# Prompt attention: the scores of a head pair on row groups of TensorE, and the order of the work around them

## The reference, cut to what matters

```python
q = (c_q @ p['w_q_b']).reshape(B, T, MLA_HEADS, QK_NOPE + QK_ROPE)
q_nope = q[..., :QK_NOPE]                  # 64 per head
q_pe = rope(q[..., QK_NOPE:], pos)         # 32 per head
q_lat = einsum('bthn,chn->bthc', q_nope, p['w_uk'])
s = (einsum('bqhc,bkc->bhqk', q_lat, ckv) + einsum('bqhr,bkr->bhqk', q_pe, kpe)) * ATTN_SCALE
s = where(k_pos <= q_pos, s, -inf)         # causal
p = softmax(s, axis=-1)
o_lat = einsum('bhqk,bkc->bqhc', p, ckv)   # then times w_uv, per head
```

## Time and profile before

| | us |
|---|---|
| median of 3 runs (lowest, highest) | 3310.39 (3306.4, 3311.9) |
| the profiled execution's own time | 3304.57 |
| its span | 3302.7 |
| prompt attention, layer 0: first scores / end of the last outputs | 927.68 / 1120.4 |
| the same stage of layer 1: first scores / last outputs begin | 2561.8 / 2754.2 |

### The profile page before, as it was taken

The page is one execution under the profiler, slowest core; times in us unless marked ns, Lnnn a source line. Parts: engine busy times, 40 slices in busy tenths (PEclk is TensorE's granted clock), DMA queues, the critical chain, the costliest instruction groups (busy, mean ns, idle before and its releaser), DMA issues. The chain is left out here.

```text
span 3302.7 us, 68611 instructions
## 1 busy us (share of the span) xinstructions
PE 3234.5 (98%) x29405; PEld 2317.0 (70%) x29405; DVE 1990.4 (60%) x3892; ACT 944.2 (29%) x2025; POOL 146.5 (4%) x168
## 2 busy tenths in 40 slices
PE   8999999999999999999999999999999999999999
PEld 5887875656666677766988878756666666777688
DVE  5545345666556778744875544466665567786565
ACT  4101013334356422221131010133333564222201
POOL 1000000000000122100000000000000001221000
PEclk8999999999999999999999999999999999999999
DMA  8122211111220377676121222111112204775431
GB/s 262 32 54 74 73 53 43 52 45 52 58 72 17 117 278 271 228 252 243 58 80 41 52 75 71 53 43 47 48 52 66 59 11 174 276 272 218 162 137 55
DMA packets 252274, 357.17 MB, mean 108 GB/s; under 512 B 47203, under 2 KB 221597, under 8 KB 243398
## 3 DMA queue, kind: packets, MB, share of 16 engines
q1 hardware_dynamic: 220166, 184.94, 18.6%
q0 software_dynamic: 15168, 151.07, 12.4%
q10 hardware_dynamic: 16640, 16.78, 1.6%
HBM read 302.17 MB, written 48.35 MB: 106 GB/s over the span
## 5 line engine op out<-in xcount | busy, mean ns | idle before, releaser
L1453 PE MATMUL ring<-u,stream_ring 128*128 128x364 f32 (+1 forms) x1728 | 613.5, 487 | 2.5 <-PEq L1324 2.5
L1453 PEld LDWEIGHTS ring<-u,stream_ring 128*128 128x128 f32 x1728 | 303.7, 189 | 150.2 <-issue 8.5
L2883 PE MATMUL dec_s_bank<-u,att_q_rows 32*64 32x256 f32 x8192 | 245.0, 386 | 0.4 <-ACT att_q_rows L2931 0.4
L2883 PEld LDWEIGHTS dec_s_bank<-u,att_q_rows 32*64 32x64 f32 x8192 | 186.8, 135 | 40.2 <-issue 12.5
L2940 ACT ACTIVATE page_probs<-dec_s_bank,dec_minus_top 128x1024 f32<-128x1024 f32 x64 | 71.4, 1115 | 338.7 <-DVE dec_minus_top L2977 338.7
L2974 DVE TENSOR_REDUCE dec_group_top<-dec_s_bank 128x1 f32<-128x1024 f32 x64 | 78.4, 1225 | 123.6 <-PE dec_s_bank L2883 123.6
L2528 PE MATMUL attn_s<-u 96*128 96x512 f32 (+3 forms) x384 | 146.2, 490 | 6.2 <-issue 3.4
L2958 DVE STREAM_TRANSPOSE u<-dec_ckv 128x2048 f32<-128x2048 f32 x52 | 116.9, 2285 | 0.7 <-DMA dec_ckv<-in_cache_mla_ckv_dram,page_row 0.7
L2166 ACT ACTIVATE rwkv_inv_x<-rwkv_inv_t 64x128 f32<-64x128 f32 x192 | 59.1, 308 | 193.4 <-DVE rwkv_inv_t L2341 191.8
L2666 DVE TENSOR_TENSOR attn_s<-attn_s,tables 128x128 f32<-128x128 f32 x128 | 38.1, 298 | 118.7 <-PE attn_s L2528 118.7
L2616 ACT ACTIVATE attn_probs_t<-ring 128x512 f32<-128x512 f32 (+2 forms) x192 | 87.1, 489 | 71.3 <-PE ring L2537 69.7
(11 more groups left out here) (745 smaller groups left out, 6566.6 us busy)
## 6 DMA issues: line engine op xcount, KB each, us to landing
stream_ring<-in_w_in_dram SPq DMA_DIRECT2D x96, 512.0 KB, 4.2
merge_sig<-gates_feature_major SPq DMA_DIRECT2D x14, 1632.0 KB, 8.3
u<-in_w_ada_dram ACTq DMA_DIRECT2D x16, 1024.0 KB, 15.1
gates_feature_major<-rwkv_gate_stage SPq DMA_DIRECT2D x72, 182.0 KB, 1.9
gates_feature_major<-rw_raw_p SPq DMA_DIRECT2D x24, 272.0 KB, 2.7
gates_feature_major<-rwkv_gate_stage SPq DMA_DIRECT2D x36, 180.0 KB, 2.0
start_ada<-in_w_ada_dram SPq DMA_DIRECT2D x6, 1024.0 KB, 13.2
x_feature_major<-o_mla SPq DMA_DIRECT2D x2, 2176.0 KB, 9.8
```

Source lines behind the costliest of these rows:

```text
L1453: mm = pe.matmul(self.banks[j % 2][:, 0:m], self.stream.w(self.first + n - self.early, k), self.s.u[:, k, t0:t0 + m], start=(k == 0), stop ...
L2883: mm = pe.matmul(S[64 * half:64 * half + NQ, 512 * i:512 * i + NK], q, keys, start=(cb == 0), stop=(cb == BLOCKS))
```

## The change

Nothing of the mathematics changes. In words:

- The plain queries of both heads lie in one tile of 128 rows (head i in rows 64 i to 64 i + 63), the plain keys too. The rotary queries of each head lie twice, in rows 64 i + 32 part; the rotary keys lie four times, in 32 rows each.
- `scores(pair)` makes both heads. The keys are halved (`n` = half of them, 64 to 512). For each half, both heads' plain products go to rows 0 to 63 and 64 to 127 of the array (two row groups). Then four rotary products (2 heads x 2 halves) go to the four row groups of 32 and accumulate on the same banks. Half y of head i is in its own PSUM bank. Each rotary matmul increments `scored`: four a pair instead of two.
- `scores(pair)` waits for the exponentials of both tiles of the pair before it, and the order of all queues is by pairs.
- Four buffers `probs` instead of two; pieces one behind each pair, two behind pair 6.
- "uk" is two full transposes instead of four half ones, "lat" two matmuls of 128 rows instead of four of 64 rows (against `q_apart`, zero outside a head's rows); ACT keeps "q" and "k" with one copy instead of two, "uk" with half as many columns.
- SP spreads the rotary queries with 8 DMAs a round instead of 4, and `scores` waits for 128 counts. POOL's four key copies no longer wait for `rope`.

```diff
-    after_tile = {0: 2, 1: 2, 2: 1, 3: 1, 4: 1, 5: 1, 6: 1}
+    after_pair = {0: 1, 1: 1, 2: 1, 3: 1, 4: 1, 5: 1, 6: 2, 7: 1}
...
@@ block.sync: spread_rope
-                        for x in range(2):
-                            sp.dma_start(q_t[r % 2][i][NOPE + x * half:NOPE + (x + 1) * half, :],
-                                         roped_q[x][h * half:(h + 1) * half, :]).then_inc(rope_in[r % 2], 16)
+                        for part in range(2):
+                            at = rope_rows(i, part).start
+                            for x in range(2):
+                                sp.dma_start(q_rope[r % 2][at + x * half:at + (x + 1) * half, :],
+                                             roped_q[x][h * half:(h + 1) * half, :]).then_inc(rope_in[r % 2], 16)
...
@@ block.tensor: scores
-                def scores(a):
-                    ...
-                    if a >= 2:
-                        pe.wait_ge(exped, a - 1)
-                    for c in range(0, (qt + 1) * P, 512):
-                        n = min(512, (qt + 1) * P - c)
-                        mm = pe.matmul(S[a % 2][:, c:c + n], q_t[r % 2][i][0:QK, qt * P:(qt + 1) * P], k_t[r % 2][i][0:QK, c:c + n],
-                                       start=True, stop=True)
-                    mm.then_inc(scored, 1)
+                def scores(pair):
+                    r, qt, _ = tiles[2 * pair]
+                    x, n = r % 2, keys_in_half(2 * pair)
+                    ...
+                        pe.wait_ge(rope_in[x], 128 * (r // 2 + 1))
+                    ...
+                        pe.wait_ge(exped, 2 * pair)
+                    for part in range(2):
+                        keys = slice(part * n, (part + 1) * n)
+                        for i in range(2):
+                            rows = rows_of_head(i)
+                            pe.matmul(S[i][:, 512 * part:512 * part + n], q_plain[x][rows, queries], k_plain[x][rows, keys], start=True, stop=False)
+                    for i in range(2):
+                        for part in range(2):
+                            rows, keys = rope_rows(i, part), slice(part * n, (part + 1) * n)
+                            pe.matmul(S[i][:, 512 * part:512 * part + n], q_rope[x][rows, queries], k_rope[rows, keys],
+                                      start=False, stop=True).then_inc(scored, 1)
...
@@ block.tensor: the order
-                for a in range(len(tiles)):
-                    if a + 2 < len(tiles):
-                        scores(a + 2)
-                    if a >= 3 and a % 2:
-                        outputs(a - 3)
-                    for p in pieces_at[a]:
-                        prologue(*p)
-                    turns(a)
+                for pair in range(N_PAIRS):
+                    if pair + 1 < N_PAIRS:
+                        scores(pair + 1)
+                    for p in pieces_at[pair]:
+                        prologue(*p)
+                    if pair:
+                        outputs(2 * pair - 2)
+                    turns(2 * pair)
+                    turns(2 * pair + 1)
...
@@ block.scalar: exponential, the order
-                    if a >= 2:
-                        act.wait_ge(ring_written, written(("turn", a - 2, len(blocks(a - 2)) - 1)))
+                    if a >= 4:
+                        act.wait_ge(ring_written, written(("turn", a - 4, len(blocks(a - 4)) - 1)))
...
-                for a in range(len(tiles)):
-                    if a + 1 < len(tiles):
-                        exponential(a + 1)
-                    ...
-                    for p in pieces_at[a]:
-                        keep(*p)
-                    keep_turned(a)
+                for pair in range(N_PAIRS):
+                    for a in (2 * pair + 2, 2 * pair + 3):
+                        if a < len(tiles):
+                            exponential(a)
+                    for p in pieces_at[pair]:
+                        keep(*p)
+                    for a in (2 * pair, 2 * pair + 1):
+                        keep_turned(a)
...
@@ block.vector: tops, the order
-                    dve.wait_ge(scored, a + 1)
+                    dve.wait_ge(scored, 2 * (a + 1))
...
-                    dve.tensor_reduce(top[:, a:a + 1], S[a % 2][:, 0:(qt + 1) * P], AX.X, ALU.max).then_inc(top_found, 1)
+                    dve.tensor_reduce(top[:, a:a + 1], halves(a), AX.XY, ALU.max).then_inc(top_found, 1)
...
-                    normalise(a)
-                    if a + 2 < len(tiles):
-                        tops(a + 2)
+                    for a in (2 * pair, 2 * pair + 1):
+                        normalise(a)
+                    for a in (2 * pair + 2, 2 * pair + 3):
+                        if a < len(tiles):
+                            tops(a)
```

More of the change, by code:

```diff
@@ L2418, in prompt_attention @@
     BEHIND = pieces.index(("v", 1))
-    after_tile = {0: 2, 1: 2, 2: 1, 3: 1, 4: 1, 5: 1, 6: 1}
+    after_pair = {0: 1, 1: 1, 2: 1, 3: 1, 4: 1, 5: 1, 6: 2, 7: 1}
     blocks = lambda a: [range(k, min(k + 4, tiles[a][1] + 1)) for k in range(0, tiles[a][1] + 1, 4)]
     ring, pieces_at = [(0, *p) for p in parts + pieces], {}
[L2423 to L2426, removed]
+    N_PAIRS = len(tiles) // 2
+    for pair in range(N_PAIRS):
+        r, at = pair // NT, pair % NT
+        first = sum(after_pair.get(x, 0) for x in range(at))
+        pieces_at[pair] = [(r + 1, *p) for p in pieces[first:first + after_pair.get(at, 0)]] if r + 1 < NP else []
+        ring += pieces_at[pair] + [("turn", a, f) for a in (2 * pair, 2 * pair + 1) for f in range(len(blocks(a)))]
     slot = {job: j for j, job in enumerate(ring)}
@@ L2436, in prompt_attention @@
         v = [ph.sb(f"v{i}", [P, NT, P]) for i in range(2)]
-        probs = [ph.sb(f"probs{i}", [P, SEQ]) for i in range(2)]
+        probs = [ph.sb(f"probs{i}", [P, SEQ])[:] for i in range(2)] + [s.o_conv[:, i, 0:SEQ] for i in range(2)]
         probs_t = ph.sb("probs_t", [P, 2, 2, SEQ])
@@ L2514, in prologue @@
-                    mm.then_inc(ring_written, 1)
-                def scores(a):
[L2517 to L2523, removed]
-                    if a >= 2:
-                        pe.wait_ge(exped, a - 1)
-                    for c in range(0, (qt + 1) * P, 512):
-                        n = min(512, (qt + 1) * P - c)
-                        mm = pe.matmul(S[a % 2][:, c:c + n], q_t[r % 2][i][0:QK, qt * P:(qt + 1) * P], k_t[r % 2][i][0:QK, c:c + n],
-                                       start=True, stop=True)
-                    mm.then_inc(scored, 1)
+                        for k in range(2):
+                            mm = pe.matmul(bank[:, 2 * k * SAMPLE:2 * (k + 1) * SAMPLE], wuk_t[:, k, :], q_apart[:].rearrange("p i n -> p (i n)"),
+                                           start=True, stop=True)
@@ L2683, in evict @@
                     dve.tensor_tensor(out, out, O[h][:], ALU.mult).then_inc(evicted, 1)
+                dve.memset(q_apart[:], 0.0).then_inc(cleared, 1)
                 rope()
@@ L2687, in _ @@
                 tops(1)
-                for a in range(len(tiles)):
-                    r, qt, i = tiles[a]
-                    normalise(a)
-                    if a + 2 < len(tiles):
-                        tops(a + 2)
-                    if 4 <= a % 16 < 6:
-                        keep_q_pe(r, a % 16 - 4)
-                    if a % 16 == 10:
+                for pair in range(N_PAIRS):
+                    r, qt, _ = tiles[2 * pair]
+                    for a in (2 * pair, 2 * pair + 1):
[3 more added lines that the diff above has]
+                            tops(a)
+                    if qt == 2:
+                        keep_q_pe(r, 0)
+                        keep_q_pe(r, 1)
+                    if qt == 5:
                         evict(2 * r)
-                    elif r and a % 16 == 2:
+                    elif r and qt == 1:
                         evict(2 * r - 1)
```

83 lines of the change are left out of this document (50 added, 33 removed).

## The result

| | before | after |
|---|---|---|
| median of the comparison's runs, us | 3310.78 (3306.4 to 3311.9, 4 runs) | 3410.91 (3405.57 to 3414.99, 4 runs) |
| ratio, 95% interval | | 1.0309 (1.0297 to 1.0322) |
| profiled execution: time, span | 3304.57, 3302.7 | 3413.24, 3411.4 |

What follows compares the result with a forecast made beforehand. The prediction took PE to bound the attention stage before the change. Cycles 33.1, DMAs 2.5, increments 1.6 and clock 2.5 made 39.7 us a layer, 79 for two: 3384 us profiled, 3390 as median, range 3340 to 3430.

Steps and rivals of the forecast that it cites:

- The cycle: Attention stage, pair by pair through PE, DVE and ACT: 56.6 us a round against 49.85, +33.1 us a layer with round 3.
- the order: Attention stage: scores of the next pair wait for both exponentials, losing look-ahead; the deciding term, inside +33.1 us a layer.
- PE's own balance: PE's work in the attention stage: 15.4 us saved by row groups, nearly all offset, leaving -2 us a layer.
- Changes of shape: PE, between matmuls of different row counts: 0.2 us a change, 16 us a layer (bounds 0 and 0.3 each).
- "uk" and "lat": PE's pieces: 12 instructions become 6 and shape changes go, saving 1 us a round, 4 a layer.
- Increments: DVE's wait for scores: two of four increments instead of one, +0.05 us a pair, +1.6 a layer (0 to 3).
- The DMAs' term: Start of the stage: first scores wait for eight rotary-query DMAs instead of four, +2.5 us a layer.
- Clock: TensorE in PE's idle stretches: a few short falls to 1.2 GHz, +2.5 us a layer (0 to 8).
- The signs: Trace after: first exponentials 56 to 57 us apart, PE busy some 165 of 233 us, DVE's waits no longer than before.
- PE stays the bound: Rival for the attention stage: other queues keep up, so only PE's work counts; 3274 to 3306 us, chance 0.14.
- Row groups that don't run side by side: Rival for the scores: row groups run one after another, +77 us a layer, 3540 us, chance 0.03.
- The clock giving way: Rival: TensorE at 1.2 GHz for most of blocks 4 to 7, +96 us, 3425 to 3490 us, chance 0.10.

Runs made afterwards that it cites:

- e6: The kernel after with matmuls that only keep PE busy, ahead of the first scores and in two pairs of round 3: 3395.21 us, ratio 1.0264 to the kernel before.
- e1: The kernel before with its own 96-row scores, but every queue in the order by pairs, with the new pieces and four probability buffers: 3345.59 us, ratio 1.0112.
- e7: The kernel before in the order by pairs, 96-row scores kept, DVE waiting until both heads' scores are out: 3429.76 us, ratio 1.0356 to the kernel before.
- e5: The kernel before with the change's "uk" and "lat" alone: 3298.86 us over 11 runs, ratio 0.9974.
- e3: The kernel after with every maximum taken twice on DVE: 3534.18 us, ratio 1.0685 to the kernel before.

## Why the prediction was right, point by point

**The cycle.** Right, pair by pair too. The table's sum for a round was 56.6 us; rounds 1 and 2 took 57.3 where the clock didn't fall. From the start of one pair's scores to the next, as the table counts, that is 5.38, 5.14, 6.39, 6.87, 8.16, 8.96, 10.68, 5.72; forecast 5.3, 5.2, 6.0, 6.9, 8.2, 9.1, 10.3, 5.6. Round 3 with each pair's shorter time of the two layers is 43.9, forecast 44.8; falls of the clock lie on both layers' third and fourth pairs, so that is a little too long. Round 0 was forecast like the others and is shorter: its first two pairs take 3.38 and 4.79 us at full clock (e6), for 5.96 and 5.82, which makes the round 53.7. Predicted +33.1 a layer; at full clock +18.9 and +11.9, 30.8.

**What the cycle is made of.** Half wrong. I named the order as the cause, and both scores ahead of DVE as given with it. e1 separates them: the order with one head after the other costs 38 us, and the row groups the rest of the cycle's growth. e7 shows that a later first head alone lengthens the cycle in this way. The formula held both, so the sum was right, the blame was not. PE's own balance (-2 us a layer) played no part.

**Changes of shape.** Right: S for 1024 keys was 1156.19 to 1159.24 with 0.16 of drain, 2.89 against the 2.96 of the formula.

**"uk" and "lat".** Right in kind: 4 us a layer forecast, e5 gives 10 us for two layers, its trace 3.6 us a layer.

**Increments.** Right in size: +1.6 a layer forecast, 1.2 measured. DVE waits for the first two of the four increments, those of head 0. In every pair of layer 0 it started 0.07 us behind the end of head 0's last instruction, where it was 0.04 in the kernel before; 0.037 us more for each of 32 pairs. The Trainium skill, "TensorE: Matmul & The Clock Gate", section on the per-tile semaphore tail, gives 0.06 us for one tile with one increment, and an estimate by its formula for four tiles and the two increments waited for is 0.10 us. The growth of 0.04 us agrees with the trace. The 0.15 us for all four, and with them the 3.0 us a layer in the prediction, no wait here shows.

**The start.** The DMAs' term was right (+2.5, measured +2.6). Missed: +6.2 until the first exponential. I had read ACT's new order and not followed it: "v" and "uk" are copied first, so the exponential waits for a value piece that PE begins only behind the scores, at half clock, and ACT's table load of 1.28 us comes behind these copies. With PE kept busy (e6) +3.9 of the 6.2 stay. And the end of the stage, +4.6, had no term: the last pair's outputs now wait for a chain that used to be ahead. Of these, 2.1 us stay in e6, at full clock.

**Clock.** Mis-sized, and the largest miss: 2.5 a layer, at most 8, where the traces give some 14. Pairs of round 3 tell the price: 11.03 us with a fall and 8.12 without for pair 5, 10.57 and 8.92 for pair 6. The 14 is an estimate: each stretch of the kernel after against the shortest at the same place in its two layers and in e6. For layer 0 and layer 1 that is 2.3 and 2.4 us up to the first exponential, 3.7 and 4.4 in rounds 0 to 2, 7.5 and 3.3 in round 3, 2.4 and 2.6 behind it: 28.7 of the 107.6 us. e6 took 16 us back. The scores of a pair with 896 keys at 1.2 GHz:

```profile
1145.37 3.36 PE L2539 MATMUL attn_s<-u 64*128 64x448 f32 x8
...
1148.66 1.78 PE L2543 MATMUL attn_s<-u 32*128 32x448 f32 x8
```

They precede a DVE turn that waits for them, so the doubled time is in the cycle. Ahead of the five transposes just before them PE had idled 2.86 us.

**The sum.** Partly luck. At full clock a layer costs 2.6 (DMAs), 3.9 (to the first exponential), 30.8 (cycles, increments included) and 2.1 (end), 39.4 us together. The forecast without its clock term was 37.2: cycles and increments 3.9 too high, start and end 6.0 too low. With the clock a layer costs 53.8, not 39.7, and the measured time lies in the range because the range had room for it above 3390.

**The signs.** First exponentials of a round 57.3 us apart, scores of a pair in 3.05 us, first scores 2.6 us later: as foreseen. PE was busy 205 of 246 us, not 165 of 233; the 84% are under the limit of 90%, and the clock of 0.91 is just over the limit of 0.9. DVE's wait for scores was to stay or shrink and grew from 59.4 to 104.0 us. With all scores of a pair ahead of it, it waits for S whole, once a pair; that was in the cycle's formula, and I drew the sign without it.

**The rivals.** That PE stays the bound is out (e3). Row groups that don't run side by side: out by the trace. The clock giving way was not a rival but a part: at least the 16 us of e6, some 29 by the estimate above.

## What to carry to other kernels

Packing products side by side on TensorE makes all of them end together: it shortens PE's work and delays the first result, and when another engine consumes results one by one the delay counts. Before pairing work up, walk one cycle through every queue and ask what each instruction now stands behind; if the pair shares a buffer that was split between its members, the look-ahead is gone. Take from such a change the parts that only remove work from the engine that bounds the stage (here 10 us), and leave its order.

## What the runs showed of the hardware

- Added matmuls made the kernel faster: 42 instructions a layer whose results nobody uses took 16 us off in all (e6). They lie in waits behind which TensorE's clock had fallen; the granted clock of the stage in layer 0 rose from 0.91 to 0.96.
- An engine that waits for the first two of four increments from four row groups started 0.07 us behind the end of the instructions, behind a single increment 0.04, behind eight 0.31.
- ACT's table load ahead of the first exponential took 1.28 us. Where it falls depends on the order of ACT's queue: in a wait in the kernel before (926.62), in the chain in the kernel after (936.39).
